# The last feed-forward block on 256 tokens: three full products per weight tile pair, or seven products over token halves

## The reference, cut to what matters

```python
def swiglu(h, w1, w3, w2):
    return (jax.nn.silu(h @ w1) * (h @ w3)) @ w2
...
        x = x + 0.5 * mx[8] * swiglu(modulate(rms_norm_2(x), mx[6], mx[7]), ffn2_w1[l], ffn2_w3[l], ffn2_w2[l])
        if not last:
            z = z + mz[5] * (mix_z @ w_out[l])
            z = z + 0.5 * mz[8] * swiglu(modulate(rms_norm_2(z), mz[6], mz[7]), ffn2_w1[l], ffn2_w3[l], ffn2_w2[l])
    return x
```

## Time and profile before

| | us |
|---|---|
| median of 3 runs | 3451.09 (3447.66 to 3451.67) |
| profiled execution, span from first to last instruction | 3451.8 |
| last feed-forward, first `f1` product to last `f2` product | 231.85 |
| of it `f1` / `f3`, 352 matmuls | 154.99 |
| of it `f2`, 176 matmuls | 76.25 |

### The profile page before, as it was taken

One profiled execution on the slowest core, in us unless ns is written; L12 is line 12 of the kernel. 1 busy time (PEld: TensorE's weight loads), 2 busy tenths in 40 slices (PEclk: granted clock), 3 DMA queues, 4 the chain that ended last, 5 costly groups with the idle time before them and its releaser, 6 DMA issues. The chain is left out here.

```text
span 3451.8 us, 41788 instructions
## 1 busy us (share of the span) xinstructions
PE 3366.7 (98%) x16652; PEld 2756.8 (80%) x16652; DVE 1621.7 (47%) x3322; ACT 578.9 (17%) x1199; POOL 23.5 (1%) x41
## 2 busy tenths in 40 slices
PE   8999999999999999999999998999999999998999
PEld 7788888888888888888886554788888888665888
DVE  5668223245673232265553574564656556455100
ACT  2121112111111122100003243100011000234100
POOL 0000000000000000000000010000000000001000
PEclk9999999999999999999999999999999999999999
DMA  6777557546876575433232221232322323222554
GB/s 194 220 208 240 175 172 207 154 140 176 221 219 219 165 201 153 116 86 98 76 96 57 67 50 35 75 111 61 92 80 74 110 62 101 62 83 39 141 160 113
DMA packets 655631, 440.69 MB, mean 128 GB/s; under 512 B 24336, under 2 KB 654512, under 8 KB 655312
## 3 DMA queue, kind: packets, MB, share of 16 engines
q1 hardware_dynamic: 652416, 430.28, 43.3%
q0 software_dynamic: 1552, 6.07, 1.1%
q10 hardware_dynamic: 1472, 1.68, 0.1%
HBM read 436.94 MB, written 1.05 MB: 127 GB/s over the span
## 5 line engine op out<-in xcount | busy, mean ns | idle before, releaser
L1850 PE MATMUL psum<-hh,ring 128*128 128x256 f32 (+2 forms) x5344 | 1260.9, 395 | 9.1 <-ACT hh L1204 5.6
L1850 PEld LDWEIGHTS psum<-hh,ring 128*128 128x128 f32 (+1 forms) x5344 | 1010.0, 191 | 235.0 <-issue 101.1
L1850 PE MATMUL psum<-arena,ring 128*128 128x256 f32 x1568 | 344.1, 383 | 6.1 <-DVE arena L1569 5.5
L1850 PEld LDWEIGHTS psum<-arena,ring 128*128 128x128 f32 x1568 | 300.9, 192 | 48.9 <-DVE arena L1569 6.3
L2041 PE MATMUL psum<-hh,ring 128*128 128x256 f32 x1056 | 246.6, 387 | 5.3 <-ACT hh L1204 5.3
L2041 PE MATMUL psum<-hh,arena 128*128 128x256 f32 x1056 | 249.0, 379 | 0.0
L2041 PE MATMUL psum<-arena 128*128 128x256 f32 x1056 | 243.1, 383 | 2.9 <-issue 1.8
L1484 DVE SCALAR_TENSOR_TENSOR arena<-arena,par 128x255 f32<-128x255 f32 (+14 forms) x480 | 225.2, 469 | 17.0
L2041 PEld LDWEIGHTS psum<-hh,ring 128*128 128x128 f32 x1056 | 202.8, 193 | 37.5 <-issue 6.0
L2064 PE MATMUL psum<-arena 128*128 128x256 f32 x1056 | 231.8, 379 | 0.0
L2041 PEld LDWEIGHTS psum<-arena 128*128 128x128 f32 x1056 | 202.5, 192 | 33.2 <-issue 3.8
(11 more groups left out here) (258 smaller groups left out, 2812.6 us busy)
## 6 DMA issues: line engine op xcount, KB each, us to landing
ring<-in_ffn_w SPq DMA_DIRECT2D x176, 512.0 KB, 5.2
ring<-in_w_mod SPq DMA_DIRECT2D x72, 1024.0 KB, 7.5
ring<-in_w_in SPq DMA_DIRECT2D x54, 1024.0 KB, 5.3
ring<-in_w_up SPq DMA_DIRECT2D x88, 512.0 KB, 5.3
ring<-in_w_in SPq DMA_DIRECT2D x84, 512.0 KB, 5.3
ring<-in_w_down SPq DMA_DIRECT2D x16, 1408.0 KB, 7.0
ring<-in_ffn_w SPq DMA_DIRECT2D x12, 1536.0 KB, 6.6
ring<-in_ffn_w SPq DMA_DIRECT2D x12, 1280.0 KB, 5.9
```

The source lines that it names most:

```text
L1850: ins = mm(o[0:rows_, 0:T], w[:, k, c0:c0 + rows_], src[:, k, 0:T], start=(k == 0), stop=(k == kt - 1))
```

## The change

The last feed-forward takes the seven-product scheme too, with the two halves of the 256 tokens (128 each) as the two column blocks. Its parts are 22 `uph` (hidden tile i of `w1` and `w3`; 7 products of 4 matmuls) and then 4 + 4 `downh` (two output tiles over hidden tiles 0 to 11 and 12 to 21; 7 products of 6 or 5 matmuls). Each matmul has 128 moving columns. Only three banks are used per part: product 0 goes to a first, product 1 to a second, product 4 to a third; products 2, 3 and 6 are accumulated one after the other on top of the first bank, product 5 on top of the third. ScalarE copies a bank's running sum to SBUF after products 0, 2, 4 and 3 (`half_copied`), and TensorE waits for that copy before it adds the next product (`HALF_AFTER`). VectorE needs three sums with 128 columns for the combination instead of seven of 256. The activations of all 22 tiles are kept (`acth`), with their sums (`ah_t1`, `ah_t3`, `ah_t4`). The four weight sums of each part are made a part ahead (`wsum`), those of the first before the last two `out` products' evictions. The first part runs its products in the order 0, 4, 1, 2, 5, 3, 6, all others 0, 1, 2, 4, 3, 5, 6.

```diff
+HALF_ORDER = (0, 1, 2, 4, 3, 5, 6)
+HALF_FIRST = (0, 4, 1, 2, 5, 3, 6)
+HALF_BANK = {2: 0, 3: 0, 6: 0, 5: 4}
+HALF_AFTER = {2: 0, 3: 2, 6: 3, 5: 4}
+HALF_COPY = {0: 0, 2: 1, 4: 2, 3: 3}
...
-    def ffn(w):
...
+    def half_ffn(w, n):
+        parts = [("uph", i) for i in range(FT)] + [("downh", g, j) for g in range(len(GROUPS)) for j in range(KT // 2)]
+        norm(n)
+        p.step("hsumh", l, w)
+        for e, part in enumerate(parts):
+            if e + 1 < len(parts):
+                p.step("wsum", l, w, *parts[e + 1])
...
+            for q in HALF_FIRST if e == 0 else HALF_ORDER:
+                p.job(*name, q, chunk=name, on=(*name, HALF_BANK[q]) if q in HALF_BANK else None)
...
+        if i == KT - 2:
+            p.step("wsum", l, 1, "uph" if last else "up7", 0)
...
+                elif kind in ("uph", "downh"):
...
+                    n = plan.halves[name]
+                    if n >= 2:
+                        evacuated(act, job[(*half_names[n - 2], 5)])
+                    for m, q in enumerate(half_copies(name)):
+                        j = job[(*name, q)]
+                        produced(act, j)
+                        do(nc.scalar.activation(copy_of(name, q), bank(j)[:, 0:HALF], ACT.Copy), half_copied, 4 * n + m + 1)
+                    if kind == "uph":
+                        evacuated(act, job[(*name, 5)])
...
+                        do(nc.scalar.activation(lead, lead, ACT.Silu), half_silu, n + 1)
...
-                        if k == half and seven(l, n):
...
+                        if k == half and n != 1:
+                            dve.wait_ge(h2_ready, scaled_count(l, n, half - 1, T // S - 1))
+                            t1 = h_t1 if seven(l, n) else hh_t1
+                            do(tt(t1, h[:, 0:half, T // 2:T], h[:, 0:half, 0:T // 2], ALU.subtract), hsum_ready,
...
+                elif kind == "hsumh":
...
+                    dve.wait_ge(h2_ready, h2_count(l, 2 * r[0]))
+                    do(tt(hh_t3, b22, b12, ALU.subtract), hsum_ready, n + 2)
+                    do(tt(b12, b22, hh_t1, ALU.subtract), hsum_ready, n + 3)
+                    do(tt(hh_t4, b21, b12, ALU.subtract), hsum_ready, n + 4)
+                elif kind in ("uph", "downh"):
...
+                    free(tt(lead[:, 0:HALF], bank(j2)[:, 0:HALF], copy_of(name, 0), ALU.add), j2)
+                    copied(dve, name, 3)
+                    do(tt(half_low, copy_of(name, 3), copy_of(name, 4), ALU.add))
+                    produced(dve, j3)
+                    free(tt(lead[:, HALF:S], bank(j3)[:, 0:HALF], copy_of(name, 2), ALU.add), j3)
+                    if kind == "uph":
...
+                        dve.wait_ge(half_silu, n + 1)
+                        do(tt(acth[:, i, HALF:S], half_low, lead[:, HALF:S], ALU.mult))
+                        produced(dve, j4)
+                        do(tt(acth[:, i, 0:HALF], bank(j4)[:, 0:HALF], lead[:, 0:HALF], ALU.mult), bank_free[bank_of(j4)], freed(j4))
...
+                    for q in order:
+                        if q in (2, 4) and order.index(q) == min(order.index(2), order.index(4)):
+                            pe.wait_ge(wsum_ready, plan.parts[name] + 1)
...
+                        if q in HALF_AFTER:
+                            copied(pe, name, HALF_AFTER[q])
+                            o = bank(j)
+                        else:
+                            o = begin(j)
+                        for k in range(n):
...
+                            ins = mm(o[:, 0:HALF], lhs[q][:, k, :], src[q][:, k, :], start=(q not in HALF_AFTER and k == 0),
+                                     stop=(k == n - 1), skip_group_check=q in HALF_AFTER)
```

More of the change, by code:

```diff
@@ L176, in step, with job @@
         self.steps.append((kind, l, *a))
-    def job(self, *name, chunk=None):
+    def job(self, *name, chunk=None, on=None):
         self.number[name] = len(self.number)
[L180 to L183, removed]
+        if on is not None:
+            self.place.append(self.place[self.number[on]])
+        else:
+            b = self.next_bank % self.ring
+            self.place.append((b, self.uses[b]))
+            self.uses[b] += 1
+            self.next_bank = b + 1
         if chunk is not None:
@@ L369, in norm @@
         p.job("spread2", l, n)
-    def ffn(w):
[L372 to L378, removed]
+    def half_ffn(w, n):
[5 more added lines that the diff above has]
+                p.step("wsum", l, w, *parts[e + 1])
+            name = (part[0], l, w, *part[1:])
+            p.parts[name] = len(p.parts)
+            p.halves[name] = len(p.halves)
+            p.step(*name)
+            for q in HALF_FIRST if e == 0 else HALF_ORDER:
+                p.job(*name, q, chunk=name, on=(*name, HALF_BANK[q]) if q in HALF_BANK else None)
     def fast_ffn(w, n):
@@ L836, in pieces @@
                 src = [(rows(a["w_mod_2"][l]), 256 * name[2], 256)]
-            elif kind == "f1":
+            elif kind in ("up7", "uph"):
                 n = name[2] + 1
                 src = [(rows(a[f"ffn{n}_w1_2"][l]), P * name[3], P), (rows(a[f"ffn{n}_w3_2"][l]), P * name[3], P)]
[L840 to L845, removed]
+            elif kind in ("down7", "downh"):
                 lo, hi = GROUPS[name[3]]
@@ L881, in weight_sums, with half_order, half_copies, copied @@
         def weight_sums(name):
-            n = KT // 2 if name[0] == "up7" else pieces(name)[0] // 2
+            n = KT // 2 if name[0] in ("up7", "uph") else pieces(name)[0] // 2
             buf = wsum[:, plan.parts[name] % 2, 0:4 * n * P]
             return buf.rearrange("p (s m c) -> p s m c", s=4, m=n)
+        def half_order(name):
+            return HALF_FIRST if name[0] == "uph" and name[-1] == 0 else HALF_ORDER
+        def half_copies(name):
+            return [q for q in half_order(name) if q in HALF_COPY]
+        def copied(eng, name, q):
+            eng.wait_ge(half_copied, 4 * plan.halves[name] + half_copies(name).index(q) + 1)
+        def copy_of(name, q):
+            n = HALF_COPY[q]
+            return half_copy[n // 2][:, plan.halves[name] % 2, n % 2, :]
+        half_names = list(plan.halves)
         def ffn_at(l, w):
```

120 lines of the change are left out of this document (80 added, 40 removed).

## The result

| | before | changed |
|---|---|---|
| median of the runs | 3451.38 us (3447.66 to 3459.14, 4 runs) | 3428.17 us (3424.15 to 3434.35, 4 runs) |
| span of the profiled execution | 3451.8 us | 3432.6 us |
| last feed-forward, first record's start to last record's end | 231.85 us | 211.22 us |

The ratio is 0.9935, with a 95% interval of 0.9923 to 0.9948: faster by 18 to 27 us, 22.4 in the middle. The forecast was 3429. The stage itself is 20.6 us shorter. Its first record starts at 3218.65 instead of 3217.24 in the profiled execution; these 1.4 us arose in code that the change does not touch. So what a variant does to the stage is read within the stage, and the medians only have to agree with it.

The account below looks back on a forecast made before the run. TensorE's matmul records were taken as the bound: first part 10.1, stall 0.75 and 1792 records at 0.1108 us give 209.4 against 231.85, so 3429 us. Forecast range 3420 to 3434 (chance 0.72); wider range 3421 to 3443.

Parts of the forecast that it names:

- Bound: Last feed-forward: pure TensorE, so time moves only with number and spacing of matmul records and gaps between products; 231.85 us.
- Spacing, the term that decides: New stage: matmul records of 128 columns start 110.8 ns apart; lower bound 106.7, upper bound 190.
- rival 1: Records in the long 128-column stream are 115 to 120 ns apart, losing 8 to 17 us: 3437 to 3445; chance 0.10.
- first step of rival 3: Records after 3227 us spaced 126 ns, as the transposes' loads seemed: stage 5 us longer than before.
- rival 3: Loads cannot run beside 128-column matmuls in steady state; slower from 123.3 ns a record, 3479 at 139, 3508 at 155; chance 0.08.
- Round trip: ScalarE's copy before a dependent product takes 0.68 to 0.75 us, hidden behind one other product with 0.14 to 0.2 spare.
- Rival 2: ScalarE's copy wait shows: 0.15 us beyond the room at 88 products costs 13 us, 3442; chance 0.07.
- VectorE and ScalarE: Their work fits beside TensorE: VectorE 10.4 of 12.4 us per two `uph` parts, ScalarE 1.7 of 6.2 per part.
- rival 4: VectorE or DMA carries the stage; 1 us above VectorE's 12.4 per two parts costs 11 us, 3440; chance 0.03.
- Start: First `uph` part takes 10.1 us; a late copy then stalls the second part by 0.75 us once.
- Other terms: 0.6 us turn before `downh` goes; end 0.35 instead of 0.48 us, +0.05; DMA at 169 GB/s costs nothing.
- Sum: Stage: 10.1 + 0.75 + 198.6 us gives 209.4 against 231.85, 22.3 less with the end: 3429.

Follow-up runs that it names:

- Experiment 7: Changed kernel with 96 instead of 128 moving columns in every matmul of the seven-product stage, the rest left out: 3428.45 us (one run).
- experiment 3: Changed kernel with ScalarE making each copy of a running sum twice, TensorE waiting for the second: 3435.63 us, ratio 0.9956.
- experiment 1: Changed kernel with 64 instead of 128 moving columns in every matmul of the seven-product stage, the rest left out: 3615.89 us (one run).
- experiment 5: Changed kernel with product order 0, 2, 1, 4, 3, 5, 6 in all parts but the first: 3452.87 us, ratio 1.0003.
- experiment 4: Changed kernel without accumulation in PSUM: seven banks per part, ScalarE copies only product 0, VectorE makes all combinations: 3443.31 us, ratio 0.9985.
- experiment 6: Changed kernel with another start: earlier silu table load, later first input difference, first part's order 0, 1, 4, 2, 5, 3, 6, earlier second-part weight sums: 3429.76 us.
- experiment 8: Kernel before, each product of its last feed-forward run as two pieces of 64 moving columns, the other columns left out: 3668.06 us (one run).

## Why the prediction was right, step by step

**Bound.** Right. In the changed kernel nothing but the number and the spacing of records sets the time after the first two parts; the chain after 3231 is one piece of TensorE.

**Spacing, the term that decides.** 110.8 ns predicted, within 110 to 111.5; 111.7 measured from start to start of a steady part (6.253 us / 56 = 111.66; 111.9 over the whole piece), 1.5 us more than the sum had over 1792 records. The value was near but its reasoning was off: it was taken nearest to the column stream (106.7 plus 3 ns, from the earlier trace rows) and the pace of the loads was used as its upper end. Experiment 7 shows that the columns add nothing, so the 111.5 of the earlier trace rows was the row to take; it would have given 210.7 instead of 209.4 for the stage, with 211.2 measured. The transposes' 126 ns of the earlier trace rows were a misreading. The first two of those eight loads alone, each 0.14 long, give this row of the kernel before:

```profile
3170.23 0.35 PEld L2230 LDWEIGHTS psum<-consts,arena 128*128 128x128 f32 x2
```

So the second starts 0.21 after the first, and the other six follow in 1.01 - 0.35 = 0.66, 0.11 each. One long first step had been spread over eight; the row spoke for a load beside a matmul of 128 columns at 110 ns, and rival 1 and the first step of rival 3 leaned on it. The 155 of the earlier trace rows did not carry over, and rival 3 (loads not beside matmuls, from 123.3 ns on) is refuted: 194-ns loads start every 112 ns.

The Trainium skill's rule ("TensorE: Matmul & The Clock Gate", Back-to-back issue gap), by which the prediction had estimated 132 ns and 15 us more than before, is not borne out here: its 25 ns on top of the columns are 5 ns in this stream (111.7 against 106.7). Another section of the same page (LDWEIGHTS) gives a load as its number of columns divided by 1.2 GHz, 106.7 ns for 128; the measured 111.9 is 5 ns above it at the full clock, and the 213.5 of experiment 1 at the lower one is twice as long.

**Round trip.** Right: hidden, and the room of 0.14 to 0.2 us was 0.20 (experiment 3 and the timeline). The sum of 0.68 to 0.75 was right for a queue that keeps streaming. Where TensorE has run dry it costs 0.78 (experiment 5), since 0.06 more pass before the load and 0.08 of lead are lost. Rival 2 was rightly feared: it needed no more than one product less in between.

**VectorE and ScalarE.** 10.4 us predicted per two parts. Measured: busy 101.47 of 132.10 us, so 9.6 of each 12.5, and 22 gaps of about 0.035 between operations, 10.4 together. Left out was the wait for the silu, 0.6 us a part, which brings it to about 11.6. It stayed free; experiment 4 shows the limit: its list has four operations more per part, 2.6 us a pair, which with the 11.6 makes the 14.2 that its pairs take, and costs 15 us in all. So 0.9 us in a pair of parts were free where the working had 2.0, and rival 4 was nearer than it looked.

**Start.** First part 10.1 us predicted, 10.13 measured (3218.65 to 3228.78, where the next part's first records start); stall of the second part 0.75 predicted, 0.65 measured (6.90 instead of 6.25). The first number holds partly by luck. The fall of the clock was not foreseen, though the earlier trace rows had a sign of it, the 0.98 over `f1`: there a record takes 154.99 / 704 = 220.2 ns, in `f2` 216.6. In the changed kernel's first part 8 records took 1.7 us from start to start instead of 0.9. Slowed down like this, product 1 ends just when VectorE has the difference that product 2 needs (3224.30), so the slow records cost nothing; experiment 6 made that list shorter and found the clock and a round trip behind it.

**Other terms.** The weight sums among the `out` evictions were free: they run from 3206.85 to 3209.72, and the eviction behind them starts at 3209.78, as its product is done. DMA: 169 GB/s predicted, 180 measured, no wait. The end: from the last record's end to the end of VectorE's last operation it is 0.57 us in both kernels, so no gain where 0.1 was counted off.

**Sum.** Predicted 209.4 us for the stage and measured 211.22: 1.8 us too little. The spacing gives 1.5 of it, the late copy in the eighth part 0.2 and the last record's full length 0.2; the stall gives 0.1 back. The time of 3428.17 lies 0.8 below the forecast although the stage is 1.8 longer; that is the spread of what lies ahead of the stage, and it is no merit of the working.

## What to carry to other kernels

When moving columns are traded for more products, count the weight loads too. Here a float32 matmul record with a 128x128 load took 216 ns with 256 columns, 112 with 128 and 112 with 96: from 128 on down, fewer columns bought nothing. A scheme that saves an eighth of the products keeps its eighth only if every dependent wait has other work of its length beside it; write down the room (here 0.2 us of 0.89) and protect it by the order of products, since one swap in the order gave all of the gain back. An engine that stays off the path should be budgeted with its waits for other engines, not with its busy time alone.

## What was not expected of the hardware

- With 64 moving columns and a load for each matmul, TensorE is recorded busy over 99% of the time, and the granted clock stays at 0.50 for 383 and 448 us (experiments 1 and 8). Why it does not rise there is open. Halving the columns of each matmul made the stage 1.9 times as long.
- The pace of the records with few columns, most likely that of their loads, follows the clock: 213.5 and 213.8 ns a record at 1.2 GHz (213.4 within a steady part of experiment 1, 11.95 us for 56), 111.7 at 2.4 GHz. Twice 106.7 is 213.4, so at the lower clock nothing is left of the 5 ns by which a record exceeds 106.7 at the full one.
- A wait that TensorE's rows name can be smaller than its cost, 0.54 for 0.78 us (experiment 5), and where the waits are short nearly nothing is named (experiment 3: 1.3 us of 8.7). The distance between the same product's starts in successive parts is the reading to trust.
